# Two attentions beside a stream of expert rows: two query blocks in one turn for tokens 0 to 255

## The chip, the cores and the metric

The kernel runs on one core of one Trainium2 chip. The metric is device microseconds of a whole execution. One execution is also taken with a hardware profiler; its times are measured from the first instruction.

## What is computed

Two blocks on 512 tokens of width 1024, in float32. The first block is a convolution and RWKV mix and then PEER: every token picks 128 of 16384 experts, each with a row of `u` and a row of `v`. The second block is one layer with differential attention (8 heads, two components of 64) and one with latent attention (8 heads), each followed by an MLP with squared ReLU.

```python
def peer_ffn(u, ...):                      # 512 tokens, 8 heads x 16 chosen experts each
    ...
    ue = jnp.take(expert_u, expert, axis=0)
    ve = jnp.take(expert_v, expert, axis=0)
    h = jax.nn.gelu(jnp.einsum('thkd,td->thk', ue, xc).astype(F32), approximate=False)
    return jnp.einsum('thk,thkd->td', (gate * h).astype(xc.dtype), ve)

def diff_attention(hn, ...):
    ...
        s = jnp.einsum('bqhcd,bkhcd->bhcqk', q_blk, k).astype(jnp.float32) * scale
        s = jnp.where(causal_mask(i, S)[None, None, None], s, -jnp.inf)
        p = jax.nn.softmax(s, axis=-1)
        a = p[:, :, 0] - lam * p[:, :, 1]
        return jnp.einsum('bhqk,bkhe->bqhe', a.astype(v.dtype), v)
    ...
def mla_attention(hn, ...):
    ...
        s = (jnp.einsum('bqhd,bkhd->bhqk', qn, k_nope)
             + jnp.einsum('bqhr,bkr->bhqk', qr, k_rope)).astype(jnp.float32) * scale
        s = jnp.where(causal_mask(i, S)[None, None], s, -jnp.inf)
        p = jax.nn.softmax(s, axis=-1)
        return jnp.einsum('bhqk,bkhe->bqhe', p.astype(v.dtype), v)
```

Both attentions are causal in blocks of 128 queries. Query blocks 0 and 1 are tokens 0 to 255, and see 128 and 256 keys.

## The kernel before, in words

Each engine has a program of its own, and engines wait for each other through named semaphores. The part in question begins when the experts of the last 256 tokens are still to be gathered. The second block is run in two halves of 256 tokens. The *first half* (`H.h` = 0) runs beside the expert rows 256 to 511, the *second half* runs alone afterwards.

A *row* is one of the 512 expert slots: GpSimd gathers 128 x 8 KB (line 1748), VectorE forms the dot product with the tokens (L1870), ScalarE applies Gelu, scales, and writes the weights as a diagonal (L1821, L1823, L1828), TensorE adds one half of the product to PSUM (L1767), VectorE the other (L1852). Seven row buffers are in use. Rows are generators, as are the stages of the first half, and `beside` draws from both on each engine:

```python
    def beside(self, stage, rows, rate):
        due = 0.0
        for weight in stage:
            self.turn += 1
            due += rate * (weight or 1)
            while due >= 1:
                next(rows, None)
                due -= 1
```

The rate is 1.1. At one step of the rows' generator ScalarE and VectorE's dot product are at row n+1, VectorE's addition at row n, and TensorE at row n-1. All engines draw the same number of steps after the same piece of a stage, so this is also the order of instructions on each engine. A group of 24 matmuls of an MLP or a projection has weight 1.

An attention stage is `attention`, which every engine runs with its own four functions (line 2126 on). Its blocks are 8 heads x 2 query blocks. In turn n come the scores of block n, the softmax of block n-1, the transposes of block n-2 ("turn") and the product with the values of block n-3 ("meet"); then it yields 1.2. `scores` on TensorE makes one PSUM tile per component in the differential attention (`pe_diff`), one tile in the latent attention (`pe_mla`), each with the causal mask added by a matmul; VectorE takes the maxima (L2428 and L2880) and scales them (L2430, L2882), ScalarE takes the exponentials (L2337, L2766), VectorE normalises (L2437 to L2444, L2887, L2889). `act_turn` copies the transposed block (L2157). At the meet ScalarE copies the output (L2347; L2776, a rounding copy called *put*), squares a finished head (L2350) or VectorE subtracts for the low part (L2895). In the first half only four PSUM banks serve the stages, in rotation (`slot`), and a tile waits until its bank's last reader is done. Exponentials and Gelu need different activation tables, so a load stands in front of each change. The blocks' exponentials have four buffers (`H.E`, `H.mE`), as have the transposed ones (`H.aT`, `H.maT`).

Behind the differential attention come the norm of its heads (matmuls L2280), the projection `w_o_a`, the MLP; then latent attention with `w_o_b` and the second MLP (`pe_mlp`), the final norm (its sums at L1992), and then the second half.

## Time and profile before

| | |
|---|---|
| runs | 3193.8, 3190.64, 3189.07 us, median 3190.64 |
| profiled execution | 3198.6 us, span 3196.8 us |
| TensorE busy | 2730.9 us (85%) |
| VectorE busy | 1994.2 us (62%) |
| GpSimd busy | 1671.4 us (52%) |
| ScalarE busy | 1444.1 us (45%) |
| rows beside the first half | 1350 to 2440 us |
| first half's differential attention | 1533 to 1634 us |
| first half's latent attention | 2049 to 2143 us |

Busy shares over the whole span mix stages with different limits; the sections below read them stage by stage. A mean clock of 1.00 means that TensorE was granted its full 2.4 GHz, 0.50 that it ran at 1.2 GHz. The second half uses the same code, but rows are over by then.

### The profile page before, as it was taken

The numbers are of one execution on the slowest core, as the hardware profiler recorded it, in microseconds if no ns is written. First come the engines' busy times: TensorE is split into PE (matmuls) and PEld (weight loads), VectorE is DVE, ScalarE is ACT, GpSimd is POOL, SyncE is SP. The second block draws the span as 40 slices with busy tenths as digits, with TensorE's granted clock in tenths as the row PEclk, the third lists the DMA queues.
The fourth block names the chain that finished last, engine by engine and source line by source line (L and its number), as shares of the span: only waits on it lengthen the run. The fifth ranks groups of instructions, "written<-read, shape, count | busy, mean of one in ns | idle before, by whom it ended". The sixth has DMA issues, their size and how long they took to land.

```text
span 3196.8 us, 43094 instructions
## 1 busy us (share of the span) xinstructions
PE 2730.9 (85%) x15302; PEld 2099.8 (66%) x15302; DVE 1994.2 (62%) x4229; ACT 1444.1 (45%) x3200; POOL 1671.4 (52%) x1014
## 2 busy tenths in 40 slices
PE   6987997798787778769889998779997999999898
PEld 3856896574333333228557776547876978998898
DVE  5685544477777777667777667767667364255423
ACT  2232222223443343345776555676554355444443
POOL 4822221283344444347447885538884607863675
PEclk8988998899999999989889998889998999999999
DMA  7210001227999999978879998889996505642454
GB/s 287 97 75 1 1 1 53 117 86 300 421 422 421 421 422 420 376 294 346 360 277 370 401 409 331 335 296 379 406 409 273 153 7 165 188 144 78 139 174 124
DMA packets 140517, 797.47 MB, mean 249 GB/s; under 512 B 15504, under 2 KB 18704, under 8 KB 67600
## 3 DMA queue, kind: packets, MB, share of 16 engines
q0 software_dynamic: 73728, 536.90, 41.4%
q1 hardware_dynamic: 65856, 253.36, 22.6%
q10 hardware_dynamic: 720, 4.46, 0.3%
q8 instruction: 123, 2.02, 0.3%
q14 instruction: 90, 0.74, 0.1%
HBM read 788.10 MB, written 6.55 MB: 249 GB/s over the span
## 4 chain that ended last, share of the span: by engine, by line
PE 46%; DMA 15%; DVE 15%; issue 8%; POOL 6%; ACT 5%; DVEq 0%; ACTq 0%; SPq 0%; POOLq 0%
PE ps L2503 8%; PE ps L1767 8%; PE ps L2522 7%; PE ps L876 6%; PE ps L1970 5%; DMA raw<-in_peer_uv,un 4%; POOL wls L299 3%; PE ps L329 3%; DVE scratch L1870 3%; DMA un<-in_peer_uv,un 2%; DMA w<-in_peer_uv,un 2%; DMA w<-in_peer_uv,scratch 2%; DMA un<-in_peer_uv,scratch 2%; POOL wlw L299 1%; POOL raw L1748 1%
## 5 line engine op out<-in xcount | busy, mean ns | idle before, releaser
L299 POOL TENSOR_TENSOR wls<-raws,whs 128x1024 fp32r<-128x1024 f32 (+1 forms) x256 | 613.7, 2407 | 381.4 <-ACT whs L293 376.8
L1767 PE MATMUL ps<-raw,un 128*128 128x512 f32 x730 | 378.7, 637 | 108.1 <-ACT un L1828 107.4
L1821 ACT ACTIVATE un<-un 128x1 f32<-128x1 f32 x512 | 103.5, 202 | 600.7 <-DVE scratch L1870 583.5
L1970 PE MATMUL ps<-ts,whs 128*128 128x256 f32 x1424 | 303.4, 314 | 28.4 <-DVE ts L2060 19.7
L299 POOL TENSOR_TENSOR wlw<-raws,whw 128x1024 fp32r<-128x1024 f32 x112 | 268.0, 2409 | 79.3 <-ACT whw L293 77.9
L1748 POOL DMA_INDIRECT raw<-in_peer_uv,un x205 | 203.3, 992 | 201.7 <-PE ps L1767 128.6
L293 ACT CAST whs<-raws 128x1024 fp32r<-128x1024 f32 (+1 forms) x256 | 263.8, 1036 | 95.8 <-PE ps L2522 34.6
L1767 PEld LDWEIGHTS ps<-raw,un 128*128 128x128 f32 x730 | 132.3, 202 | 251.6 <-ACT un L1828 169.7
L1970 PEld LDWEIGHTS ps<-ts,whs 128*128 128x128 f32 x1424 | 242.1, 205 | 59.8 <-issue 35.5
L2522 PE MATMUL ps<-ts,whs 128*128 128x256 f32 x1216 | 240.7, 299 | 0.0
L1870 DVE SCALAR_TENSOR_TENSOR scratch<-raw,ps 128x1024 f32<-128x1024 f32 x149 | 181.1, 1216 | 94.3 <-DMA raw<-in_peer_uv,un 90.9
L1767 PE MATMUL ps<-un 128*128 128x512 f32 x364 | 197.2, 658 | 45.7 <-ACT un L1828 39.5
L1767 PE MATMUL ps<-w,un 128*128 128x512 f32 x376 | 187.9, 640 | 50.1 <-ACT un L1828 50.1
L1828 ACT ACTIVATE un<-kept,un 128x128 f32<-128x128 f32 x512 | 205.8, 402 | 50.1 <-ACT un L1823 1.9
L2503 PE MATMUL ps<-ts,whw 128*128 128x256 f32 x960 | 192.6, 301 | 20.8 <-DVE ts L2060 20.8
L1970 PE MATMUL ps<-ts,wls 128*128 128x256 f32 x712 | 210.1, 295 | 0.0
L2503 PE MATMUL ps<-ts,whs 128*128 128x256 f32 x1088 | 209.9, 294 | 0.0
L2522 PEld LDWEIGHTS ps<-ts,whs 128*128 128x128 f32 x1216 | 193.4, 192 | 22.2 <-issue 21.5
L299 POOL TENSOR_TENSOR wl<-raw,wh 128x2048 fp32r<-128x2048 f32 x23 | 106.8, 4651 | 171.7 <-ACT wh L293 171.7
L2503 PEld LDWEIGHTS ps<-ts,whs 128*128 128x128 f32 x1088 | 171.4, 191 | 14.9 <-issue 14.2
L2503 PEld LDWEIGHTS ps<-ts,whw 128*128 128x128 f32 x960 | 155.5, 196 | 36.9 <-DVE ts L2060 23.1
L1767 PEld LDWEIGHTS ps<-w,un 128*128 128x128 f32 x376 | 71.7, 202 | 160.8 <-ACT un L1828 92.7
(442 smaller groups left out, 7104.8 us busy)
## 6 DMA issues: line engine op xcount, KB each, us to landing
raws<-in_w_up SPq DMA_DIRECT2D x128, 512.0 KB
raws<-in_w_down SPq DMA_DIRECT2D x128, 512.0 KB
scratch<-in_ada_w SPq DMA_DIRECT2D x17, 1024.0 KB, 13.3
raws<-in_w_qk SPq DMA_DIRECT2D x32, 512.0 KB
raw<-in_w_in SPq DMA_DIRECT2D x11, 1024.0 KB, 6.1
raw<-in_peer_w_q SPq DMA_DIRECT2D x8, 1024.0 KB, 7.9
raws<-in_w_v SPq DMA_DIRECT2D x16, 512.0 KB
raws<-in_w_o_a SPq DMA_DIRECT2D x16, 512.0 KB
```

Of the source, the lines that this page charges most:

```text
L293: e.copy(self.wh[h][:, 0:width], self.raw[slot][:, 0:width]).then_inc(*self.tick("hi", key))
L299: e.tensor_tensor(self.wl[h][:, 0:width], self.raw[slot][:, 0:width], self.wh[h][:, 0:width].bitcast(F32), ALU.subtract).then_inc(*self.ti ...
L329: ins = e.matmul(self.ps[:, b, :], l, r, start=k == 0 and i == 0, stop=k == nk - 1 and i == 2)
L876: ins = e.matmul(self.ps[:, b, 128 * q:128 * q + 128], l, r, start=n == 0, stop=n == len(terms) - 1)
L1748: e.indirect_dma_start(self.rows[r], None, self.d["peer_uv"], index).then_inc(*self.tick(f"row{r}", n, 16))
L1767: ins = e.matmul(self.ps[:, b + half, :], self.diag[n % 4], self.rows[self.row_of(n)][:, 1024 + 512 * half:1536 + 512 * half], start=k == ...
L1821: e.activation(self.gelus[:, c], self.dots[:, c], ACT.Gelu, bias=0.0, scale=1.0).then_inc(*self.tick(S))
L1828: e.activation(self.diag[n % 4], self.C("ident"), ACT.Identity, bias=0.0, scale=self.weight[:, c]).then_inc(*self.tick(S, ("diag", n)))
L1870: e.scalar_tensor_tensor(out=self.junk[n % 2 if n < 256 else 1], in0=self.rows[r][:, 0:1024], scalar=1.0, in1=xn, op0=ALU.mult, op1=ALU.mu ...
L1970: ins = e.matmul(o[:, 0:256], l, r, start=k == 0 and i == 0, stop=k == nk - 1 and i == 2)
L2503: ins = e.matmul(o[:, 0:256], l, r, start=k == 0 and n == 0, stop=k == 7 and n == 2)
L2522: ins = e.matmul(o[:, 0:256], l, r, start=t == 0 and n == 0, stop=t == 3 and n == 2)
```

## The change

For the first half alone, a head's two query blocks go through the attention in one turn. `pairs` has 11 turns of weight 2.4 in place of 19 of weight 1.2. Both blocks' scores of a component lie in one PSUM tile (128 + 256 columns); one wait on either side covers both. The maxima are written side by side and scaled by one instruction; the reciprocals are one instruction. The three transposes of a head go to one PSUM tile and are copied by one instruction of 384 columns; the output of a head is copied (and, in the latent attention, subtracted) in one instruction of 256 columns. Exponentials and normalisations remain one per block and component. The buffers of exponentials serve two heads in place of four blocks. The second half keeps `attention`. Since `beside` draws rows per weight, the rows move as well.

```diff
@@ -2137,8 +2139,48 @@
             yield 1.2
 
     @staticmethod
-    def nothing(n, hh, qb):
+    def nothing(*block):
         return None
+
+    def pairs(self, scores, softmaxed, turn, meet):
+
+        for n in range(11):
+            if n < 8:
+                scores(n)
+            if 1 <= n <= 8:
+                softmaxed(n - 1)
+            if 2 <= n <= 9:
+                turn(n - 2)
+            if n >= 3:
+                meet(n - 3)
+            yield 2.4
+
+    def pe_pair_turn(self, e, S, n, blocks, A_, D_):
+
+        o, before = self.slot((S, "turn", n), (A_, ("turn", n)))
+        for f in before:
+            e.wait_ge(*self.at(*f))
+        e.wait_ge(*self.at(D_, ("soft", n)))
+        for i, a in enumerate((blocks[0][:, 0:128], blocks[1][:, 0:128], blocks[1][:, 128:256])):
+            ins = e.transpose(o[:, 128 * i:128 * i + 128], a, self.C("ident"))
+        ins.then_inc(*self.tick(S, ("turn", n)))
+
+    def act_pair_turn(self, e, S, n, aT, P_):
+        if n >= 2:
+            e.wait_ge(*self.at(P_, ("meet", n - 2)))
+        e.wait_ge(*self.at(P_, ("turn", n)))
+        e.copy(aT, self.bh((P_, "turn", n), 384)).then_inc(*self.tick(S, ("turn", n)))
+
+    def pe_pair_meet(self, e, S, n, v, aT, A_, freed):
+        o, before = self.slot((S, "meet", n), freed)
+        for f in before:
+            e.wait_ge(*self.at(*f))
+        e.wait_ge(*self.at(A_, ("turn", n)))
+        for q, kb in ((0, 0), (1, 0), (1, 1)):
+            c = 128 * (q + kb)
+            ins = e.matmul(o[:, 128 * q:128 * q + 128], v[:, kb, 128 * n:128 * n + 128], aT[:, c:c + 128], start=kb == 0,
+                           stop=kb == q)
+        ins.then_inc(*self.tick(S, ("meet", n)))
...
     def queries(self, H, qb):
...
-        yield from self.attention(H, scores, self.nothing, turn, meet)
+        def pair_scores(n):
+            for c in range(2):
+                p = slice(64 * c, 64 * c + 64)
+                o, freed = self.slot((S, "score", n, c), (A_, ("exp", n, c)))
+                for f in freed:
+                    e.wait_ge(*self.at(*f))
+                if n == 0 and c == 0:
+                    e.wait_ge(*self.at(D_, ("roped", 15)))
+                for qb in range(2):
+                    w, at = 128 * (qb + 1), 128 * qb
+                    e.matmul(o[:, at:at + w], H.q[p, n, 128 * qb:128 * qb + 128], H.k[p, n, 0:w], start=True, stop=False)
+                    ins = e.matmul(o[:, at + 128 * qb:at + w], self.C("ident"), self.C("causal"), start=False, stop=True)
+                ins.then_inc(*self.tick(S, ("score", n, c)))
+
+        def pair_turn(n):
+            self.pe_pair_turn(e, S, n, H.E[2 * (n % 2):2 * (n % 2) + 2], A_, D_)
+
+        def pair_meet(n):
+            if n == 0:
+                e.wait_ge(*self.at(D_, ("w_v", 3, 0)))
+                e.wait_ge(*self.at(A_, ("w_v", 3, 1)))
+            self.pe_pair_meet(e, S, n, H.v, H.aT2[n % 2], A_, (A_, ("o", n)))
+
+        if h:
+            yield from self.attention(H, scores, self.nothing, turn, meet)
+        else:
+            yield from self.pairs(pair_scores, self.nothing, pair_turn, pair_meet)
...
-        yield from self.attention(H, scores, self.nothing, turn, meet)
+        def pair_scores(n):
+            if n == 0:
+                e.wait_ge(*self.at(P_, ("w_v", 3, 1)))
+            if n >= 2:
+                e.wait_ge(*self.at(P_, ("turn", n - 2)))
+            e.wait_ge(*self.at(D_, ("max", n)))
+            st = small[:, 104 + 16 * (n % 2):120 + 16 * (n % 2)]
+            for c in range(2):
+                for qb in range(2):
+                    w, at, i = 128 * (qb + 1), 128 * qb, 8 * c + 4 * qb
+                    e.activation(H.E[2 * (n % 2) + qb][:, 256 * c:256 * c + w],
+                                 self.bh((P_, "score", n, c), at + w)[:, at:at + w], ACT.Exp, bias=st[:, i + 1:i + 2], scale=0.125,
+                                 accum_out=st[:, i + 2:i + 3]).then_inc(*self.tick(S, ("exp", n, c) if qb else None))
+
+        def pair_turn(n):
+            self.act_pair_turn(e, S, n, H.aT2[n % 2], P_)
+
+        def pair_meet(n):
+            e.wait_ge(*self.at(P_, ("meet", n)))
+            e.copy(H.o[:, n, :], self.bh((P_, "meet", n))).then_inc(*self.tick(S, ("o", n)))
+            e.wait_ge(*self.last(S))
+            e.activation(H.q[:, n, :], H.o[:, n, :], ACT.Square, bias=0.0, scale=1.0).then_inc(*self.tick(S, ("sq", n)))
+
+        if h:
+            yield from self.attention(H, scores, self.nothing, turn, meet)
+        else:
...
-        yield from self.attention(H, scores, softmaxed, self.nothing, self.nothing)
+        def pair_scores(n):
+            st = small[:, 104 + 16 * (n % 2):120 + 16 * (n % 2)].rearrange("p (g k) -> p g k", k=4)
+            for c in range(2):
+                e.wait_ge(*self.at(P_, ("score", n, c)))
+                for qb in range(2):
+                    w, at = 128 * (qb + 1), 128 * qb
+                    e.tensor_reduce(st[:, 2 * c + qb, 0:1], self.bh((P_, "score", n, c), at + w)[:, at:at + w], AX,
+                                    ALU.max).then_inc(*self.tick(S))
+            e.wait_ge(*self.last(S))
+            e.tensor_scalar(st[:, :, 1], st[:, :, 0], -0.125, None, ALU.mult).then_inc(*self.tick(S, ("max", n)))
+
+        def pair_softmaxed(n):
+            st = small[:, 104 + 16 * (n % 2):120 + 16 * (n % 2)].rearrange("p (c q k) -> p c q k", q=2, k=4)
+            blocks = [(qb, 128 * (qb + 1), H.E[2 * (n % 2) + qb]) for qb in range(2)]
+            e.wait_ge(*self.at(A_, ("exp", n, 1)))
+            e.reciprocal(st[:, :, :, 3], st[:, :, :, 2]).then_inc(*self.tick(S))
+            e.wait_ge(*self.last(S))
+            e.tensor_scalar(st[:, 1, :, 3], st[:, 1, :, 3], nl, None, ALU.mult).then_inc(*self.tick(S))
+            e.wait_ge(*self.last(S))
+            for qb, w, ee in blocks:
+                e.tensor_scalar(ee[:, 256:256 + w], ee[:, 256:256 + w], st[:, 1, qb, 3:4], None, ALU.mult).then_inc(*self.tick(S))
+            for qb, w, ee in blocks:
+                e.wait_ge(*self.last(S, 1 - qb))
+                e.scalar_tensor_tensor(out=ee[:, 0:w], in0=ee[:, 0:w], scalar=st[:, 0, qb, 3:4], in1=ee[:, 256:256 + w],
+                                       op0=ALU.mult, op1=ALU.add).then_inc(*self.tick(S, ("soft", n) if qb else None))
+
+        if h:
+            yield from self.attention(H, scores, softmaxed, self.nothing, self.nothing)
+        else:
+            yield from self.pairs(pair_scores, pair_softmaxed, self.nothing, self.nothing)
...
-        yield from self.attention(H, scores, self.nothing, turn, meet)
-        yield from self.tail_gemm(e, H, "w_o_b", lambda k: H.A[k], lambda k: (D_, ("put", 2 * k + 1)), S,
...
+            for qb in range(2):
+                w, at, qs = 128 * (qb + 1), 128 * qb, slice(128 * qb, 128 * qb + 128)
+                e.matmul(o[:, at:at + w], H.qn[:, n, qs], H.kn[:, n, 0:w], start=True, stop=False)
+                e.matmul(o[:, at:at + w], H.qr[:, n // 2, qs], H.kr[:, n % 2, 0:w], start=False, stop=False)
+                ins = e.matmul(o[:, at + 128 * qb:at + w], self.C("ident"), self.C("causal"), start=False, stop=True)
+            ins.then_inc(*self.tick(S, ("score", n)))
...
+        if h:
+            yield from self.attention(H, scores, self.nothing, turn, meet)
+        else:
+            yield from self.pairs(pair_scores, self.nothing, pair_turn, pair_meet)
+        yield from self.tail_gemm(e, H, "w_o_b", lambda k: H.A[k], lambda k: (D_, ("put", 2 * k + 1 if h else k)), S,
...
+        def pair_scores(n):
+            st = small[:, 104 + 8 * (n % 2):112 + 8 * (n % 2)]
+            if n >= 2:
+                e.wait_ge(*self.at(P_, ("turn", n - 2)))
+            e.wait_ge(*self.at(D_, ("max", n)))
+            for qb in range(2):
+                w, at = 128 * (qb + 1), 128 * qb
+                e.activation(H.mE[2 * (n % 2) + qb][:, 0:w], self.bh((P_, "score", n), at + w)[:, at:at + w], ACT.Exp,
+                             bias=st[:, 4 * qb + 1:4 * qb + 2], scale=192.0 ** -0.5,
+                             accum_out=st[:, 4 * qb + 2:4 * qb + 3]).then_inc(*self.tick(S, ("exp", n) if qb else None))
...
     def dve_mla(self, e, H):
...
+        def pair_scores(n):
+            st = small[:, 104 + 8 * (n % 2):112 + 8 * (n % 2)].rearrange("p (q k) -> p q k", k=4)
+            e.wait_ge(*self.at(P_, ("score", n)))
+            for qb in range(2):
+                w, at = 128 * (qb + 1), 128 * qb
+                e.tensor_reduce(st[:, qb, 0:1], self.bh((P_, "score", n), at + w)[:, at:at + w], AX,
+                                ALU.max).then_inc(*self.tick(S))
+            e.wait_ge(*self.last(S))
+            e.tensor_scalar(st[:, :, 1], st[:, :, 0], -(192.0 ** -0.5), None, ALU.mult).then_inc(*self.tick(S, ("max", n)))
...
+        def pair_softmaxed(n):
+            st = small[:, 104 + 8 * (n % 2):112 + 8 * (n % 2)].rearrange("p (q k) -> p q k", k=4)
+            e.wait_ge(*self.at(A_, ("exp", n)))
+            e.reciprocal(st[:, :, 3], st[:, :, 2]).then_inc(*self.tick(S))
+            e.wait_ge(*self.last(S))
+            for qb in range(2):
+                w, ee = 128 * (qb + 1), H.mE[2 * (n % 2) + qb]
+                e.tensor_scalar(ee[:, 0:w], ee[:, 0:w], st[:, qb, 3:4], None,
+                                ALU.mult).then_inc(*self.tick(S, ("soft", n) if qb else None))
+
+        def pair_meet(n):
+            e.wait_ge(*self.at(A_, ("put", n)))
+            e.tensor_tensor(H.A[n][1], self.bh((P_, "meet", n)), H.A[n][0].bitcast(F32),
+                            ALU.subtract).then_inc(*self.tick(S, ("put", n)))
+
+        if h:
+            yield from self.attention(H, scores, softmaxed, self.nothing, meet)
+        else:
+            yield from self.pairs(pair_scores, pair_softmaxed, self.nothing, pair_meet)
```

ScalarE's instructions in the middle of the first half's differential attention. `e` are exponentials, `at` and `ap` the transposed blocks, `o` and `q` the output and its squares; L1821, L1823 and L1828 together are a row. Before, a turn of a 128-key block:

```order
L2337 ACT_TABLE_LOAD
L2337 ACTIVATE e_111,kept<-ps,kept 128x128 x2
L2157 COPY at_113<-ps 128x128
L2347 COPY o_100<-ps 128x128
L2350 ACTIVATE q_97<-o_100 128x256
L1821 ACT_TABLE_LOAD
L1821 ACTIVATE un<-un 128x1
L1823 ACTIVATE un<-un 128x1
L1828 ACTIVATE un<-kept,un 128x128
```

After the change, from the load to the second row of the same turn:

```order
L2430 ACT_TABLE_LOAD
L2430 ACTIVATE e_109,kept<-ps,kept 128x128
L2430 ACTIVATE e_110,kept<-ps,kept 128x256
L2430 ACTIVATE e_109,kept<-ps,kept 128x128
L2430 ACTIVATE e_110,kept<-ps,kept 128x256
L2172 COPY ap_117<-ps 128x384
L2439 COPY o_100<-ps 128x256
L2441 ACTIVATE q_97<-o_100 128x256
L1821 ACT_TABLE_LOAD
L1821 ACTIVATE un<-un 128x1
L1823 ACTIVATE un<-un 128x1
L1828 ACTIVATE un<-kept,un 128x128
```

Four exponentials now stand behind one load, and two or three rows behind the other. The whole program has 74 table loads where it had 106.

TensorE in the same place (L1767 is a row, L2258 and L2259 or L2325 and L2326 scores and mask, L2152 or L2165 transposes, L2166 or L2181 the product with the values). Before:

```order
L2258 MATMUL ps<-k_98,q_97 128x256
L2259 MATMUL ps<-kept 128x128
L2258 MATMUL ps<-k_98,q_97 128x256
L2259 MATMUL ps<-kept 128x128
L2152 MATMUL ps<-kept,e_112 128x128 x2
L2166 MATMUL ps<-at_115,v_99 128x128
L1767 MATMUL ps<-scratch,un 128x512
L2258 MATMUL ps<-k_98,q_97 128x128
```

After:

```order
L2326 MATMUL ps<-kept 128x128
L2165 MATMUL ps<-kept,e_111 128x128
L2165 MATMUL ps<-kept,e_112 128x128 x2
L2181 MATMUL ps<-ap_117,v_99 128x128 x3
L1767 MATMUL ps<-un 128x512 x2
L1767 MATMUL ps<-raw_64,un 128x512
L2325 MATMUL ps<-k_98,q_97 128x128
L2326 MATMUL ps<-kept 128x128
```

Where one row stood between two turns' scores, three stand here.

TensorE at the last row. Before, in `mlp1` (L2522, its last value matmuls) and the final norm:

```order
L2522 MATMUL ps<-ts_90,whw_83 128x256 x2
L2522 MATMUL ps<-ts_90,wlw_84 128x256
L1767 MATMUL ps<-raw_64,un 128x512
L1992 MATMUL ps<-gel_91,kept 128x256
L1787 MATMUL ps<-kept,un 128x128 x8
```

After:

```order
L2645 MATMUL ps<-ts_90,whw_83 128x256 x2
L2645 MATMUL ps<-ts_90,wlw_84 128x256
L1767 MATMUL ps<-raw_64,un 128x512
L2645 MATMUL ps<-ts_90,whw_83 128x256 x2
L2645 MATMUL ps<-ts_90,wlw_84 128x256
```

The last row has moved ahead of the MLP's last 180 matmuls.

## Rows read from the trace of the kernel before

**Rows 1.** The page's first line.

```profile
span 3196.8 us, 43094 instructions
```

**Rows 2.** Stretches: from:to, length, busy us and instructions per engine, clock, DMA share, GB/s.

```profile
1541.70:1624.00 82.30, 65.83 (x208) 36.24 (x209) 63.93 (x190) 73.48 (x173) 17.85 (x19) 0.77 0.83 321
2054.00:2134.00 80.00, 51.98 (x183) 31.20 (x181) 50.67 (x130) 69.68 (x149) 20.39 (x22) 0.84 0.85 321
2200.00:2400.00 200.00, 191.70 (x1300) 163.05 (x1299) 134.81 (x261) 111.77 (x261) 167.13 (x103) 1.00 1.01 406
2680.00:2840.00 160.00, 160.00 (x1335) 160.00 (x1334) 44.70 (x113) 73.74 (x110) 128.69 (x55) 1.00 0.60 183
```

**Rows 3.** Line L2337, 1534 to 1636 us: ns min/median/max, first and last start.

```profile
L2337 ACT ACT_TABLE_LOAD  x16: 1283/1283/1283, 1537.2 to 1623.1; - x16
```

**Rows 4.** Line L2766, 2049 to 2146 us.

```profile
L2766 ACT ACT_TABLE_LOAD  x16: 1283/1283/1283, 2053.1 to 2132.2; - x16
```

**Rows 5.** ScalarE in order of time, first stage: start, us taken, instruction.

```profile
1580.23 0.47 ACT L2337 ACTIVATE e<-ps,kept 128x256 f32<-128x256 f32 x1
...
1581.14 0.37 ACT L2157 COPY at<-ps 128x256 f32<-128x256 f32 x1
1581.39 0.28 ACT L2347 COPY o<-ps 128x128 f32<-128x128 f32 x1
1581.69 1.28 ACT L1821 ACT_TABLE_LOAD   x1
1582.99 0.20 ACT L1821 ACTIVATE un<-un 128x1 f32<-128x1 f32 x1
...
1584.04 0.20 ACT L1821 ACTIVATE un<-un 128x1 f32<-128x1 f32 x1
...
1586.43 0.37 ACT L2337 ACTIVATE e<-ps,kept 128x128 f32<-128x128 f32 x1
...
1587.13 0.26 ACT L2157 COPY at<-ps 128x128 f32<-128x128 f32 x1
```

**Rows 6.** VectorE in order of time, first stage; in brackets the idle time before.

```profile
1600.20 0.75 DVE L1852 SCALAR_TENSOR_TENSOR ps<-un,ps 128x512 f32<-128x512 f32 x1 [0.66 <-ACT un L1823]
1600.86 0.42 DVE L2428 TENSOR_REDUCE kept<-ps 128x1 f32<-128x256 f32 x1
1601.31 0.15 DVE L2430 TENSOR_SCALAR kept<-kept 128x1 f32<-128x1 f32 x1
...
1602.40 0.29 DVE L2442 TENSOR_SCALAR e<-e,kept 128x128 f32<-128x128 f32 x1
...
1602.99 1.21 DVE L1870 SCALAR_TENSOR_TENSOR scratch<-raw,ps 128x1024 f32<-128x1024 f32 x1
...
1604.13 0.75 DVE L1852 SCALAR_TENSOR_TENSOR ps<-un,ps 128x512 f32<-128x512 f32 x1
```

**Rows 7.** TensorE in order of time, first stage, at the lower and the upper clock.

```profile
1543.67 0.79 PE L2258 MATMUL ps<-k,q 64*128 64x128 f32 x2
1544.39 0.79 PE L2259 MATMUL ps<-kept 128*128 128x128 f32 x2
...
1596.82 1.02 PE L1767 MATMUL ps<-scratch,un 128*128 128x512 f32 x2
1597.78 0.70 PE L2258 MATMUL ps<-k,q 64*128 64x256 f32 x2
1598.40 0.49 PE L2259 MATMUL ps<-kept 128*128 128x128 f32 x2
1598.82 0.70 PE L2258 MATMUL ps<-k,q 64*128 64x256 f32 x2
```

**Rows 8.** VectorE in order of time, second stage: the subtraction behind the put.

```profile
2095.07 0.29 DVE L2895 TENSOR_TENSOR ts<-ps,ts 128x128 fp32r<-128x128 f32 x1 [1.73 <-ACT ts L2776]
```

**Rows 9.** TensorE in order of time: the first matmuls behind the two stages.

```profile
1636.68 0.60 PE L2280 MATMUL ps<-q,kept 128*8 128x256 f32 x2
...
2143.36 0.80 PE L1970 MATMUL ps<-ts,whs 128*128 128x256 f32 x2
```

**Rows 10.** TensorE in order of time, where the rows end.

```profile
2437.88 1.02 PE L1767 MATMUL ps<-raw,un 128*128 128x512 f32 x2
2444.02 1.22 PE L1992 MATMUL ps<-gel,kept 128*128 128x256 f32 x2 [5.12 <-DVE gel L2051]
```

26 lines of the change are left out of this document (24 added, 2 removed).

## The prediction

> **What bounds the kernel now.** I read first the table of stretches: the two attention stages of the first half of the tokens (1533 to 1634 us and 2049 to 2143 us), the expert rows beside the MLP (2200 to 2400) and the same MLP code in the second half, without rows (2680 to 2840). Beside the MLP the DMA engines are full (share 1.01, 406 GB/s) and TensorE is busy 191.7 of 200 us; in the two attention stages ScalarE is the fullest engine (73.48 of 82.3 us and 69.68 of 80 us), the DMA share is 0.83 and 0.85, and the mean TensorE clock is 0.77 and 0.84 [rows 2]. Then I read the pace of the attention turns: sixteen Exp table loads from 1537.2 to 1623.1 us are 15 gaps of 5.73 us; in the second stage 2053.1 to 2132.2 gives 5.27 us [rows 3, 4]. Then one turn of ScalarE: two exponentials of 256 columns 0.91 us (1580.23 to 1581.14), two copies 0.55 (to 1581.69), a table load 1.30 to the next start (to 1582.99), a row's three activations 1.05 (to 1584.04), and at 128 columns the exponentials take 0.70 (1586.43 to 1587.13) [rows 5]. With the Exp load of 1.30 that is 5.1 us for a turn with one row and 6.2 with two, which is the measured pace: the first stage runs at ScalarE's sum, half of it table loads. The second adds a loop through VectorE, which waits 1.73 us in a turn for ScalarE's cast [rows 8].
>
> The program's time is 3198.6 us for a span of 3196.8 [rows 1]; sums are made against 3198.6, and their result is taken off the median of the runs, 3190.6, which lies 8 us lower.
>
> **The change, part by part.** Per attention stage, 19 turns of weight 1.2 become 11 of weight 2.4. At 1.1 rows per weight the stage carries 29 rows instead of 25. The rows are drawn after a turn's work, so they now stand in bunches of 3 or 2 where there were 1 or 2. Between the eight Exp loads of the first stage they are 3, 2, 3, 3, 2, 3, 3, and in the second 2, 3, 3, 2, 3, 3, 2.
>
> *ScalarE's own sum.* A pair of turns costs 2 x 5.73 = 11.5 us. A joint turn keeps all exponentials (0.91 + 0.70), has one load of each table (2.6), one copy of 384 and one of 256 columns (an estimate of 0.66 from 0.28 to 0.37 us for 128 and 256 columns [rows 5]), the square (0.43) and 2.64 rows at 1.05 (2.8): 8.1 us. All in all 32 table loads go. What a load costs is the 1.30 us from its start to the next activation's [rows 5]. The Trainium skill, page "ScalarE: Activation LUTs", section "What ACT_TABLE_LOAD costs", adds about 1.38 us of drain to each 1.28 us load. By that 32 loads would give back some 44 us more, as an estimate from the page; the trace does not agree, since the activation behind the load starts 1.30 us after it and the copy before it ends as it starts, so nothing is counted for it.
>
> *What is late next: the first stage.* TensorE works two rows behind ScalarE. In a bunch of two both its rows were made ready in the turn before, but the third of a bunch needs the diagonal that ScalarE makes first in this same bunch, behind load, exponentials, copies and the Gelu load. On TensorE the next turn's scores are queued behind it. From the moment the maxima are ready: 1.3 + 1.6 + 1.1 + 1.3 + 1.0 = 6.3 us to that diagonal; its matmul 0.96 (1596.82 to 1597.78); the scores, per component 0.42 and 0.62 us for 128 and 256 columns and 0.42 twice for the mask, 1.87, twice 3.74 [rows 7]; the last maximum and its scaling, with handovers, 1.0 (0.42 and 0.15 are the ops [rows 6]). That is 12.0 us at the upper clock level. While it waits TensorE stands still for 4 us in a row, and at the lower level a step of 0.42 takes 0.72 (1543.67 to 1544.39) [rows 7]. I add 1.0 for part of the scores at that level: 13.0. A bunch of two is bound by VectorE, which waits for the weight of the bunch's first row, as it does today for 0.66 us behind a table load [rows 6]: 5.8 + 0.66 + 1.4 for maxima = 7.9, taken 8.2. Seven gaps: 5 x 13.0 + 2 x 8.2 = 81.4 against 85.9 [rows 3]: -4.5. Bounds: VectorE's path alone (9.7 and 7.9) gives 64.3, -21.6; the lower clock throughout (15.6 and 10.3) gives 98.6, +12.7.
>
> *The first stage's end.* From the last maxima to the matmuls of the sub-norm (1636.68 [rows 9]) stand four turns' rows and those of the weight 2 behind: 7.5 rows now, 12.8 then. Now it is 13.0 us, and VectorE does a row in 1.80 us (1.14 from 1602.99 to 1604.13 and 0.66 behind it [rows 6]). 5.3 more rows are 9.5 us; waiting once for ScalarE and the wider last softmax, with its 128-column part at 0.59 us (1602.40 to 1602.99 [rows 6]), 2.9 more. A row is 128 x 8 KB, 2.6 us at 406 GB/s [rows 2], and twelve in a line outrun it: +2 (0 to 8). The first maxima come 2 us later, since a component now has both blocks' scores ahead of them. Stage: -4.5 + 12.4 + 2 + 2 = +11.9.
>
> *The second stage.* No scores wait for an exponential's bank here, and they are 1.8 us a pair. The loop is ScalarE to the put (1.3 + 0.8 + 0.65 = 2.75), the joint subtraction 0.35, rows at 1.80, maxima and scaling 0.85: 9.4 for three rows, 7.5 for two; by TensorE's third row 5.0 + 0.96 + 1.8 + 0.9 = 8.7 and up to 10.7 at the lower clock. I take 9.9 and 7.5: 4 x 9.9 + 3 x 7.5 = 62.1 against 79.1 [rows 4]: -17.0 (-20 to -12). Its end, from the last maxima at 2132 to the first matmul of w_o_b at 2143.36 [rows 9], is 11.3 us now with 5.3 rows and 22.8 with 10.6, two of them hidden behind the put: +11.4; +1.3 for start and supply. Stage: -4.3.
>
> *The second MLP's end.* Both stages take 8 rows off it: behind the last row TensorE has 180 weight matmuls where it had none, 7.5 groups of 24. With rows a group takes 4.03 us (1300 records in 200 us, 108 of them rows'), without 2.88 (1335 in 160) [rows 2]: 7.5 x 1.15 = -8.6. At the seam the norm's sums start 6.0 us after the last value matmul (2437.9 to 2444.02 [rows 10]); the last row's VectorE work (1.8) and its sums' copy on ScalarE leave that wait, the slow adds beside GpSimd stay: -3.4 (0 to -4.5). Together -12.0.
>
> *Nothing* is counted for the second half, whose attention is untouched, for the stores of keys and values (same place), and for GpSimd's splits, which follow the same spots. If more rows per turn made GpSimd issue late, the DMA's free share in the stages (0.83, 0.85) covers some 15% and no more.
>
> Sum: +11.9 - 4.3 - 12.0 = **-4.4 us**, 3194.2 on the profiled execution's scale and 3186 on the runs'.
>
> **Rivals.** *A, the third row holds nobody.* If TensorE's last row of a bunch finds its diagonal ready, or its delay is hidden by VectorE, the first stage runs on VectorE's path, 17 us less: 3169. For it: VectorE's sum is itself 8 to 9.7, and ScalarE's 8.1. Against: ScalarE can't reach the row before two loads. *B, TensorE's clock makes it slower.* The still stretches of 4 us in five of seven turns keep the clock at its lower level while the scores, now on the path, run: +17 in the first stage and +4 in the second, 3207. For it: the level is lower already for almost half of the first stage (0.77) [rows 2]. It is slower than before from 13.9 us per three-row turn on. Against: TensorE is busy for 8 us behind each wait. *C, the merged work does not matter,* because rows keep the pace by DMA: at 2.6 us a row the stage's 29 rows need 75 us, less than the 100 it takes, so only ends and starts are touched; 3194. That the change doesn't do what it says is ruled out by the order of instructions: 74 table loads stand where 106 stood.
>
> **How the numbers follow.** My forecast 0.50, A 0.24, B 0.18, C 0.08. A measurement tells about 0.2%, 6.4 us, from no change. The forecast's own spread (3179 to 3195) lies one third beyond -6.4. So faster 0.24 + 0.17 = 0.41; slower 0.18 + 0.02 = 0.20; the same 0.39. The range, 3168 to 3204, leaves out 0.2 at its ends.
>
> **What would show it.** In the changed kernel's first stage: Exp loads 12 to 13.5 us apart where three rows lie between, 8 where two do; TensorE idle for 3 to 4 us before the third row of a bunch, with ScalarE's diagonal as the releaser; ScalarE no longer over 90% busy; VectorE working rows back to back for over 20 us behind the last exponential; in the second stage 9.9 and 7.5. The last row about 20 us before the second MLP's end. If the three-row gaps are under 11 us the third row is not the bound and A holds; if over 14, B. It is wrong as a whole if the MLP's matmuls after the last row don't run at 2.9 us per 24.

## The result: slower, because the next scores queue behind a late row and then run at the lower clock

The changed kernel takes 3209.3 us (median of 13 runs, 3198.7 to 3214.2) where the kernel before takes 3198.3 (13 runs, 3189.1 to 3205.2): 1.0028 times as long, 95% interval 1.0018 to 1.0039. I had forecast a gain of 4.4 us, to 3186 us, starting from the 3190.6 us that the first three runs of the kernel before gave; its thirteen runs give 3198.3, so 7.7 of the 23 us between 3186 and 3209.3 are not of the change, and the changes themselves, -4.4 and +9 us, are compared below. The profiled execution took 3211.3 us against 3198.6. Of all runs behind this document one is set aside, 5262.8 us for e12, whose other five lie between 3159.7 and 3169.3 with a median of 3166.3.

Page of the changed kernel, its first lines; the busy times beside those of the table before the change:

```profile
span 3209.5 us, 42886 instructions
...
PE 2739.1 (85%) x15302; PEld 2111.0 (66%) x15302; DVE 1984.3 (62%) x4149; ACT 1398.6 (44%) x3136; POOL 1676.0 (52%) x1014
```

ScalarE is indeed 45 us less busy (1444.1 before), 41 of them its 32 table loads of 1.28 us, and the kernel is slower all the same. To see where, I followed instructions that both kernels have and noted how much later each starts:

| instruction | before | after | later by | in this piece | forecast |
|---|---|---|---|---|---|
| projections ahead of the first stage | 1435.8 | 1440.9 | 5.1 | | |
| first matmul of the sub-norm | 1636.7 | 1660.6 | 24.0 | +18.9 | +11.9 |
| first MLP's start (L2503) | 1684.2 | 1711.0 | 26.8 | +2.8 | 0 |
| ahead of the second stage | 2048.2 | 2068.0 | 19.8 | -7.0 | 0 |
| first matmul of `w_o_b` | 2143.4 | 2165.6 | 22.2 | +2.4 | -4.3 |
| last value matmul of the second MLP | 2438.0 | 2451.8 | 13.8 | -8.4 | -8.6 |
| behind the seam | 2501.6 | 2514.0 | 12.4 | -1.4 | -3.4 |

The 5.1 us ahead of the stage is in code that the change doesn't touch, and is scatter of executions: in ten of the twelve kernels below the same place is 2.4 to 6.6 us later than in this execution of before, in two 0.8 and 1.2. What is left is +7.3 us, which agrees with the ratio's 9 within the interval's 3. Forecast were -4.4. Both attention stages are worse than forecast by 7 us each, and the MLP's end is right.

The loads of the Exp table in the changed kernel, first and second stage (number of loads, first and last start; before: [rows 3, 4]):

```profile
L2430 ACT ACT_TABLE_LOAD  x8: 1283/1283/1283, 1543.7 to 1635.7; - x8
...
its engine sat idle before it (us, times) until:
  DVE kept L2556: 28.7, 6
```

```profile
L2933 ACT ACT_TABLE_LOAD  x8: 1283/1283/1283, 2073.4 to 2140.8; - x8
```

Seven gaps take 92.0 us in the first stage (14.3, 7.9, 15.4, 15.5, 8.1, 16.1, 14.6) and 67.4 in the second (5.5, 12.8, 10.7, 7.7, 12.0, 11.0, 7.7). The short ones are those with two rows (and the first of the second stage, 5.5). ScalarE, 89% busy in the stage before (73.48 of 82.30 us [rows 2]), now sits idle for 28.7 us ahead of its loads until VectorE has the scaled maxima (the profile names L2556, the instruction next to the scaling L2550). Who is it that makes them late? One turn of three rows, first ScalarE:

```profile
1581.36 1.28 ACT L2430 ACT_TABLE_LOAD   x1 [7.22 <-DVE kept L2556]
...
1585.48 1.28 ACT L1821 ACT_TABLE_LOAD   x1
...
1587.39 0.40 ACT L1828 ACTIVATE un<-kept,un 128x128 f32<-128x128 f32 x1
...
1596.87 1.28 ACT L2430 ACT_TABLE_LOAD   x1 [6.59 <-DVE kept L2556]
```

TensorE in the same turn (start, us taken, in brackets the idle time ahead of the instruction and what ended it):

```profile
1582.12 3.37 PE L1767 MATMUL ps<-un 128*128 128x512 f32 x4
1587.85 1.44 PE L1767 MATMUL ps<-raw,un 128*128 128x512 f32 x2 [2.35 <-ACT un L1828]
1589.22 0.79 PE L2325 MATMUL ps<-k,q 64*128 64x128 f32 x2
1589.94 0.79 PE L2326 MATMUL ps<-kept 128*128 128x128 f32 x2
...
1595.13 0.79 PE L2326 MATMUL ps<-kept 128*128 128x128 f32 x2
1595.72 0.85 PE L2165 MATMUL ps<-kept,e 128*128 128x128 f32 x3
```

Two rows run at 1582.12, the third only at 1587.85, when ScalarE has made its diagonal (L1828, 1587.39), and the next scores behind it from 1589.22 to 1595.72. A step of 128 columns takes 0.72 us (1589.22 to 1589.94), what it took at the lower clock level before [rows 7]. The stretches of these scores in the first and in the second stage (columns as in [rows 2]; the granted clock is the third number from the end):

```profile
1589.20:1595.70 6.50, 6.50 (x17) 4.06 (x17) 1.31 (x5) 0.90 (x3) 0.94 (x1) 0.50 0.81 308
2117.50:2120.80 3.30, 3.30 (x13) 2.94 (x12) 1.24 (x3) 0.90 (x3) 0.94 (x1) 0.50 0.97 340
```

Both ran at 0.50, 1.2 GHz, behind a row for which TensorE had stood idle. So did the scores of the other three-row turns of the first stage: 0.50 over three of them, 0.57 over the last (1628.6 to 1634.5), behind waits of 3.4 to 4.9 us. In the second stage the other three read 0.65 to 0.71. Behind the two rows of a short turn the scores ran at 1.00 and 0.98 (1600.0 to 1603.7, 1561.1 to 1564.7).

### The profile page after: what moved, and what is told of

It is laid out like the page before. It is cut to its first block, busy times and chain, and to the rows that moved or that the text cites. A ratio compares the mean times of both kernels' runs of the same rounds, so it can differ in the third digit from the quotient of the medians.

```text
span 3209.5 us, 42886 instructions
## 1 busy us (share of the span) xinstructions
PE 2739.1 (85%) x15302; PEld 2111.0 (66%) x15302; DVE 1984.3 (62%) x4149; ACT 1398.6 (44%) x3136; POOL 1676.0 (52%) x1014
## 4 chain that ended last, share of the span: by engine, by line
PE 48%; DMA 14%; DVE 14%; POOL 7%; issue 6%; ACT 5%; DVEq 0%; ACTq 0%; SPq 0%; POOLq 0%
PE ps L1767 8%; PE ps L2645 7%; PE ps L2626 7%; PE ps L876 6%; PE ps L1972 6%; DMA raw<-in_peer_uv,un 4%; POOL wls L299 3%; PE ps L329 3%; DMA un<-in_peer_uv,un 3%; DVE scratch L1870 2%; DMA raw<-in_peer_uv,scratch 2%; DMA w<-in_peer_uv,un 2%; POOL wlw L299 1%; DMA w<-in_peer_uv,scratch 1%; DMA un<-in_peer_uv,scratch 1%
## 5 line engine op out<-in xcount | busy, mean ns | idle before, releaser
L1767 PE MATMUL ps<-raw,un 128*128 128x512 f32 x730 | 381.7, 643 | 114.5 <-ACT un L1828 113.4
L1821 ACT ACTIVATE un<-un 128x1 f32<-128x1 f32 x512 | 103.4, 202 | 597.7 <-DVE scratch L1870 586.1
L1972 PE MATMUL ps<-ts,whs 128*128 128x256 f32 x1424 | 304.9, 315 | 27.5 <-DVE ts L2062 18.9
L1767 PEld LDWEIGHTS ps<-raw,un 128*128 128x128 f32 x730 | 133.9, 203 | 263.8 <-ACT un L1828 174.4
L1767 PE MATMUL ps<-un 128*128 128x512 f32 x364 | 194.4, 652 | 64.7 <-ACT un L1828 61.2
L1767 PE MATMUL ps<-w,un 128*128 128x512 f32 x376 | 188.6, 642 | 51.2 <-ACT un L1828 51.1
L1828 ACT ACTIVATE un<-kept,un 128x128 f32<-128x128 f32 x512 | 205.8, 402 | 48.6 <-ACT un L1823 1.5
L2626 PEld LDWEIGHTS ps<-ts,whs 128*128 128x128 f32 x1088 | 172.4, 192 | 15.3 <-issue 14.1
L2725 DVE TENSOR_TENSOR kept<-kept,ps 128x256 f32<-128x256 f32 x256 | 104.0, 417 | 123.4 <-PE ps L2645 123.1
```

The lines of the kernel that those rows point to most:

```text
L1767: ins = e.matmul(self.ps[:, b + half, :], self.diag[n % 4], self.rows[self.row_of(n)][:, 1024 + 512 * half:1536 + 512 * half], start=k == ...
L1821: e.activation(self.gelus[:, c], self.dots[:, c], ACT.Gelu, bias=0.0, scale=1.0).then_inc(*self.tick(S))
L1828: e.activation(self.diag[n % 4], self.C("ident"), ACT.Identity, bias=0.0, scale=self.weight[:, c]).then_inc(*self.tick(S, ("diag", n)))
L1972: ins = e.matmul(o[:, 0:256], l, r, start=k == 0 and i == 0, stop=k == nk - 1 and i == 2)
L2626: ins = e.matmul(o[:, 0:256], l, r, start=k == 0 and n == 0, stop=k == 7 and n == 2)
L2725: e.tensor_tensor(x, x, self.bh((P_, "v", g, j)), ALU.add).then_inc(*self.tick(S, ("x", g, j)))
```

## Experiments

Each is stated against the kernel before, which ran beside it on the same chip (4 to 12 runs each); medians of before lay between 3199.0 and 3200.8 us. Where the text compares two of these kernels, or one of them with the changed kernel, it takes their medians; by the ratios such a difference can come out about 2 us smaller.

| kernel | median us | ratio, 95% |
|---|---|---|
| e1: joint turns in the first stage alone | 3216.8 | 1.0056 (1.0041 to 1.0071) |
| e2: joint turns in the second stage alone | 3198.8 | 0.9995 (0.9981 to 1.0008) |
| e3: scores ahead of the rows on TensorE | 3179.8 | 0.9942 (0.9927 to 0.9957) |
| e4: TensorE kept busy while it waits | 3198.2 | 1.0000 (0.9989 to 1.0012) |
| e5: the kernel before, with the moved rows | 3201.6 | 1.0003 (0.9994 to 1.0013) |
| e6: two rows a turn | 3180.6 | 0.9945 (0.9929 to 0.9962) |
| e7: e3 with transposes earlier too | 3176.8 | 0.9931 (0.9914 to 0.9949) |
| e8: rows drawn at two places of a turn | 3201.6 | 1.0005 (0.9996 to 1.0014) |
| e9: e7 and two rows a turn | 3182.8 | 0.9950 (0.9935 to 0.9965) |
| e10: e7 with few rows in the last turns | 3180.6 | 0.9937 (0.9920 to 0.9955) |
| e11: e9 with rate 1.13 | 3171.8 | 0.9918 (0.9901 to 0.9936) |
| e12: two rows a turn, rate 1.13, order as changed | 3166.6 | 0.9903 (0.9884 to 0.9922) |

### Which stage: e1 and e2

For one of the attentions the branch of the second half is taken in both halves:

```diff
-        if h:
+        if True:
             yield from self.attention(H, scores, self.nothing, turn, meet)
```

> The joint turns in the differential attention alone; the latent attention has its 19 single turns as before. The profiled changed kernel lost 18.9 us up to the end of the first stage, gave 6.7 back in the MLP behind it, and lost 2.4 net in the second stage. If the losses add up stage by stage, this kernel ends 8 to 12 us behind the kernel before (the MLP's end gives back half of what it gave, since only 4 rows are moved ahead). If the give-back in the first MLP is DMA work caught up, it is seen here too, 5 to 8 us. If the 4 rows moved are what counts, this kernel and the one with the second stage alone come out alike.

> The joint turns in the latent attention alone. If the stages add up: second stage +2, the end of the second MLP -5 (4 rows instead of 8 moved ahead of it), so 1 to 5 us ahead of the kernel before. If bunching itself costs something outside its stage (late gathers), it is no better than the kernel before.

e2 can't be told from the kernel before, and so does not choose between its two expectations. e1 is much worse than expected: 18 us behind the kernel before where 8 to 12 were. The stage itself repeats (+20.4 us in e1, +18.9 in the changed kernel), so the loss is the first stage's. The surprise is the second MLP: with 8 rows moved ahead of its end the changed kernel gained 8.4 us there, with 4 rows e1 gained 0.9 and e2 1.8, not half. So the two parts don't add up (+0.56% and -0.05% against +0.28% for both). Why four rows bring so little I didn't find out.

### What the third row's place costs: e3

TensorE alone puts the next head's scores ahead of the rows; the order of its other instructions, and the rotation of PSUM banks, stay.

```diff
+            if n < 8 and not (ahead and n):
                 scores(n)
...
                 meet(n - 3)
+            if ahead and n < 7:
+                scores(n + 1)
             yield 2.4
```

> The changed kernel, with TensorE's order alone altered: the scores of the next head stand ahead of a turn's rows, not behind them. ScalarE and VectorE keep their order. Theory (TensorE's third row waits for ScalarE's diagonal, the next scores are queued behind it and then run at the lower clock): the three-row gaps between Exp loads fall from 15.3 to about 10 us in the first stage and from 11.7 to about 9.5 in the second, the wait before the third row goes, the clock of the first stage rises from 0.71 to over 0.85, and the kernel is 30 us faster than the changed one, some 20 us faster than before. Rival (rows come late from the gathers, or VectorE's order is the bound): the gaps fall by under 2 us each and the kernel stays at or behind the kernel before.

It is 0.58% faster than before (18.6 us), 29.5 us faster than the changed kernel (medians), as the theory said. The loads of its first stage and TensorE in one turn:

```profile
L2432 ACT ACT_TABLE_LOAD  x8: 1283/1283/1283, 1543.1 to 1613.9; - x8
```

```profile
1596.42 0.49 PE L2327 MATMUL ps<-k,q 64*128 64x128 f32 x2 [0.33 <-ACT e L2432]
...
1599.76 0.49 PE L2328 MATMUL ps<-kept 128*128 128x128 f32 x2
1600.08 1.02 PE L1767 MATMUL ps<-raw,un 128*128 128x512 f32 x2
1600.94 1.02 PE L1767 MATMUL ps<-scratch,un 128*128 128x512 f32 x2
1601.80 1.02 PE L1767 MATMUL ps<-un 128*128 128x512 f32 x2
```

```profile
1596.40:1600.00 3.60, 3.58 (x16) 2.32 (x17) 0.86 (x2) 3.51 (x10) 0.00 (x0) 1.00 0.99 357
```

The gaps sum to 70.8 us instead of 92.0 (59.8 instead of 67.4 in the second stage). The scores take 3.7 us at the full clock, three rows follow without a wait. One part of what I expected failed: the stage's mean clock rose from 0.72 to 0.81 only; it still reads 0.50 from 1559 to 1574 and for about 5 us each from 1589, 1609 and 1624.

And two gaps did not move, the first with three rows in each stage: 14.3 us, as in the changed kernel, and 12.1 (12.8 there). VectorE waits there for the gathers of its rows, 3.43 and 4.27 us in the first stage, 3.08 and 1.86 in the second, and its maxima stand behind these rows:

```profile
1555.11 1.22 DVE L1870 SCALAR_TENSOR_TENSOR scratch<-raw,ps 128x1024 f32<-128x1024 f32 x1 [4.27 <-DMA raw<-in_peer_uv,un]
...
1556.91 1.14 DVE L2549 TENSOR_REDUCE kept<-ps 128x1 f32<-128x128 f32 x4
```

The changed kernel has the same waits (4.26 us at 1555.7, 3.96 at 2085.4), so in these two turns late gathers alone would have held the turn nearly as long.

### What of it is the clock: e4

Ahead of a bunch's third row TensorE runs five matmuls of 256 columns into the tile that the next scores overwrite.

```diff
             while due >= 1:
+                if drawn == 2 and self.fill:
+                    self.fill()
                 next(rows, None)
...
+                for _ in range(5):
+                    e.matmul(o[:, 128:384], H.q[0:64, n - 1, 128:256], H.k[0:64, n - 1, 0:256], start=True, stop=True)
```

> The changed kernel, with five matmuls of 256 columns added on TensorE ahead of the third row of a bunch, while it waits (they write the tile that the next scores overwrite, so they change nothing else). If the lower clock is what stretches the scores from 3.74 to 6.5 us, TensorE now keeps the upper level, the three-row gaps of the first stage fall from 15.3 to 12.5 to 13.5 us, and the whole falls by 8 to 15 us though work was added. If the clock is not the cause, the gaps stay at 15.3 or grow by up to 1 us.

With work added the kernel fell by 11 us (9 by the ratios), to the time of the kernel before. TensorE in one such turn; L1773 is the row, L2345 the added work:

```profile
1604.19 2.42 PE L2345 MATMUL ps<-k,q 64*128 64x256 f32 x10
1606.78 1.12 PE L1773 MATMUL ps<-un 128*128 128x512 f32 x2 [0.17 <-ACT un L1834]
1607.84 0.48 PE L2333 MATMUL ps<-k,q 64*128 64x128 f32 x2
...
1611.17 0.49 PE L2334 MATMUL ps<-kept 128*128 128x128 f32 x2
1611.50 0.49 PE L2173 MATMUL ps<-kept,e 128*128 128x128 f32 x3
```

The scores take 3.7 us (1607.84 to 1611.50) instead of 6.5. Its gaps are 13.8, 8.1, 15.4, 12.3, 8.1, 12.3, 14.7 in the first stage: in two of the five three-row turns the scores ran at 1.00, and these take 12.3; in the other three they ran at 0.50 to 0.55 all the same. In the second stage the seven gaps take 60.7 us instead of 67.4. So the same order costs 12.3 us a turn at the upper level and 15.4 at the lower; e3, with the order mended, 9.1 to 11.3 behind its first turn. That splits the excess of a three-row turn: about 3 us are the clock, 1 to 3 the order.

### The moved rows by themselves: e5

```diff
-            yield 1.2
+            yield 1.2 if H.h else 1.39
```

> The kernel before with its single turns, their weight 1.39 in place of 1.2 in the first half: 29 rows instead of 25 in each stage, singly and in twos, and the last row ahead of the second MLP's last 180 matmuls, as in the changed kernel. By the terms of my sum: a row more costs a stage ScalarE's 1.05 us, so +4 to +5 in each stage, about +3 at each stage's end (VectorE's 1.8 us a row), and the second MLP's end gives 8.6 back: 3 to 8 us slower than before. If moving rows forward is worth more than it costs, it is faster by 2 to 5 us.

No difference (+0.03%, interval -0.06 to +0.13), which is neither of the two expectations. In the profile the gaps of the stages grow by 2.4 and 6.3 us and their ends by 1.9 each, 12.5 in all, and the second MLP is 7.5 us shorter, the first 5 (of which, as shown further below, 3 may be scatter). So the rows that a stage takes on are paid back behind it. The loss isn't the four rows; it is how they stand.

### No third row: e6 and e8

```diff
-            yield 2.4
+            yield 1.82
```

> The changed kernel with the joint turn's weight 1.82 in place of 2.4: exactly two rows behind each turn, 22 rows a stage, none that is a third of its bunch; six rows fewer than before stand in the stages, and they stand behind the second MLP. If the third row is what makes a turn long, all gaps between Exp loads are near 8.0 us, the first stage is 35 to 45 us shorter than in the changed kernel (its end 4 to 5 of that), the second 15 to 20, the rows left behind the MLP cost 11 to 16 us and the MLP's row-free tail of 8.6 is lost: 20 to 35 us faster than the changed kernel. If joint turns are long for another reason (clock, supply, VectorE), the gaps are 10 us and more and it is slower than the changed kernel.

```diff
                 softmaxed(n - 1)
+            yield 1.2
             if 2 <= n <= 9:
...
                 meet(n - 3)
-            yield 2.4
+            yield 1.2
```

> The changed kernel with the turn's weight given in two parts of 1.2, one ahead of the transposes and products and one behind them: the same 29 rows, but in ones and twos, never three in a row. If the bunch as such is what costs, the gaps fall to 9 or 10 us and the whole by 20 us or more. If it is the wait of TensorE's third row of a turn for the diagonal that ScalarE makes first in the same turn, wherever it stands, only the copies (1.3 us) leave that wait: the three-row gaps fall from 15.3 to 14 us, the whole by 3 to 10 us against the changed kernel.

e6 has no third row in a turn, and is 28.7 us faster than the changed kernel. Its loads:

```profile
L2430 ACT ACT_TABLE_LOAD  x8: 1283/1283/1283, 1543.3 to 1603.6; - x8
```

The gaps are 7.3, 11.8, 7.3, 8.1, 9.0, 8.1, 8.7, together 60.3. The scores of the long one did run at the lower level, but they were done at 1559.4, and what VectorE's maxima (1561.06) wait for is a gather that comes 2.85 us late:

```profile
1559.25 1.22 DVE L1870 SCALAR_TENSOR_TENSOR scratch<-raw,ps 128x1024 f32<-128x1024 f32 x1 [2.85 <-DMA raw<-in_peer_uv,un]
```

In the second stage five of seven are 9.3 or 7.7. A third row in a turn had thus made it 7 us longer in the first stage, 4 in the second. The first stage is 36 us shorter than in the changed kernel, as expected, the second 22, somewhat more. (The profiled execution, 3167.3 us, is the fastest of e6's six; their median is 3180.6.)

e8 keeps all 29 rows but never three in a row. It gained 8 us on the changed kernel. Its gaps in the first stage are 13.9, 8.2, 15.1, 11.4, 7.4, 15.3, 11.4: in the turns of 15.1 and 15.3 TensorE still waits 4.3 and 3.5 us for ScalarE's diagonal and runs the scores at the lower level; in the two of 11.4 it keeps the upper one, which I had not expected (14 us for all of them). The wait of the first:

```profile
1566.74 2.08 PE L1767 MATMUL ps<-scratch,un 128*128 128x512 f32 x2 [4.30 <-ACT un L1823]
1568.75 0.79 PE L2326 MATMUL ps<-k,q 64*128 64x128 f32 x2
```

So it is the dependence within a turn, not the bunch.

### What bounds the mended turn: e7, e9 and e10

e7 also puts a head's transposes one turn earlier on TensorE, behind the scores:

```diff
+            if ahead and 1 <= n <= 8:
+                turn(n - 1)
             yield 2.4
```

> The kernel with the scores ahead of the rows (3179.8 us), and on TensorE the transposes of a head one turn earlier, behind the next head's scores and ahead of the rows. There ScalarE waited 1.48 us in a turn with its Exp table loaded, until TensorE had done the transposes behind the last rows, and VectorE 2.88 us for ScalarE. If that wait is on the path, the three-row gaps fall from 9.1 to 11.3 to about 9.7 and less, 1 to 1.5 us a turn in both stages together 8 to 12 us. If VectorE's own sum (9.4 to 9.7 us) is the bound already, under 3 us.

> Both remedies at once: scores and transposes ahead of the rows on TensorE, and two rows behind each joint turn (22 a stage). If two-row turns of 8 us are ScalarE's sum (two loads, exponentials, copies, two rows: 7.6 us), only the turns of 9.0 and 11.8 us in the first stage of the two-row kernel, where TensorE ran at its lower level, get shorter: 2 to 8 us faster than 3180.6. If VectorE's wait for the transposes and weights counts too, 10 us and more. If the rows left to the MLPs are paced by the DMA engines, nothing.

e10 is e7 with

```diff
-            yield 2.4
+            yield 2.73 if n < 8 else 0.91
```

> The kernel with scores and transposes ahead of the rows (3176.8 us), its first eight turns with weight 2.73 (three rows each) and the last three, which have no new scores, with 0.91 (one row each): 27 rows a stage, 8 instead of 12 to 13 behind the last maxima. By VectorE's 1.8 us a row the stages' ends fall from 28.3 and 24.6 to about 20 and 17 us, the two gaps of 7.7 grow to 9.7, and four rows more beside the second MLP cost 4.3: 2 to 8 us faster. If the ends are not VectorE's rows, no change.

e7 can't be told from e3 (the intervals overlap). Its three-row gaps behind the first turn are 9.1 to 10.0: VectorE's sum of three rows, softmax and maxima, the second of the two expectations. e9 gained nothing on e6: its first-stage gaps (7.9, 11.7, 7.4, 8.1, 8.7, 8.2, 8.2) are the same, the long second one too, where VectorE waits 2.68 us for a gather. With two rows a turn the order no longer matters.

e10 missed. The ends did fall, from 28.3 and 24.6 us to 17.2 and 14.1, but the kernel didn't get faster than e7 (3180.6 and 3176.8 us). The gaps grew by 2.5 and 6.7, the second MLP by 6.4 us. Rows taken out of the uncovered end are paid for where they go.

### A better version: e11 and e12

```diff
-RATE = 1.1
+RATE = 1.13
...
-            yield 2.4
+            yield 1.775
```

This is e12 against the changed kernel; e11 is e9 with the same two numbers.

> The same with the general rate 1.13 instead of 1.1 and the joint turn's weight 1.775 (still two rows a turn): the six rows that stood behind the second MLP are spread over projections and MLPs, and the last row stands at the MLP's end, as before the change. If the MLPs' pace is that of the DMA engines, which carry every row somewhere, only the bare rows behind the MLP go: 3 to 8 us faster than the same kernel with rate 1.1. If a row more costs an MLP the 2.6 us that it takes at 406 GB/s, the gain is nothing or a loss of up to 6 us.

> The changed kernel with two numbers altered and its order kept: the joint turn's weight 1.775 (two rows a turn) and the general rate 1.13. Two-row turns have no third row, and the orders with and without the early scores came out alike at two rows (3182.8 and 3180.6 us), so this should equal the kernel with both (3171.8 us) within 0.2%. If the early scores still shorten turns once the rows are spread anew, it is 6 us or more behind that kernel.

e6 and e9 leave six rows behind the second MLP, where nothing covers them. With the rate at 1.13 they stand beside projections and MLPs. e11 gained 11 us on e9, more than the 3 to 8 expected, and e12, the changed kernel with only these two numbers altered, is at 3166.6 us the fastest: 0.97% faster than before (interval 0.78 to 1.16), and not told apart from e11 (their intervals overlap). Its loads in both stages:

```profile
L2430 ACT ACT_TABLE_LOAD  x8: 1283/1283/1283, 1543.6 to 1602.3; - x8
```

```profile
L2933 ACT ACT_TABLE_LOAD  x8: 1283/1283/1283, 2037.6 to 2087.6; - x8
```

Gaps of 58.7 and 50.0 us in sum, against 86.0 and 79.0 before, with 22 rows in each stage where before had 25. So the joint turn with two rows and the rate 1.13 is a good change; with the weight that came with it, it was not. How much of the 0.97% is the joint turn's is not shown: the single turns with rate 1.13 and fewer rows in the stages were not run. e5 shows only that more rows in the stages gain them nothing.

## Right and wrong, step by step

**ScalarE's sum: right.** The exponentials, copies and loads up to the second table load took 4.1 us (1581.36 to 1585.48; forecast 1.3 + 1.6 + 1.1). In a turn with two rows ScalarE is busy for 7.1 of 8.1 us (1596.87 to 1604.97); my terms, 8.1 us for 2.64 rows, give 7.4 for two. So its sum is right, and it is nearly the bound of a two-row turn, as VectorE's path is.

**The third row waits: right, in place and size.** From the load to the row's start 6.5 us (forecast 6.3 to the diagonal), the scores queued behind. TensorE is idle ahead of the third row for 4.8, 4.7, 2.35, 4.9 and 3.4 us in the five turns of the first stage, 4.0 on average (forecast 3 to 4); the turn shown above has the shortest, since its first two rows took 3.37 us at the lower clock.

**Two-row gaps: right.** 7.9 and 8.1 us in the first stage (8.2), 5.5, 7.7, 7.7 in the second (7.5).

**Three-row gaps: the step that failed.** I wrote the path at the upper clock level, 12.0, and added "1.0 for part of the scores at that level". The scores ran at the lower one, in four of the five turns from first to last and in the fifth but for their first microsecond. The terms as measured in the turn shown: 6.5 to the diagonal, 1.4 the row's matmul (0.96), 6.5 the scores (3.74 + 1.0), 1.15 maxima and scaling (1.0), in sum 15.5. The five gaps average 15.2, so the stage's gaps are 92.0, not 81.4: 10.6 us of the whole distance of 11.7 between forecast and result. The second stage's gaps add 5.3 (67.4 against 62.1), and the other misses take 4.2 off. The order of the step was right and its size was not: the term of the scores, 4.7 us forecast, measured 6.5. This is rival B, for whose gaps I had 15.6; its two-row gaps of 10.3 didn't come. It gave 3207, as change +16, where +9 was measured. I gave it 0.18, and argued that TensorE is busy for 8 us behind each wait. It was busy, but at the lower level: the clock came back only when the scores were over (it reads 0.50 up to 1598 and 1.00 from 1599 on). In the second stage the turn with the slowest scores has 5.6 to the diagonal's use, 1.9 the row (0.96), 3.4 the scores (1.8), 1.15, in sum 12.0, where I took 9.9. The four three-row gaps average 11.6; one of them, 12.8, is one of the two with late gathers, where VectorE waits 3.96 and 1.65 us for its rows. I had counted nothing for gathers between the loads of a stage; the other such turn is the first of the first stage, 14.3.

**The stages' ends: right in the first, short by 2 in the second.** 25.0 us now and 13.5 before, +11.5 where I had 12.4 and 2 for the gathers; 24.8 and 11.2, +13.6, in the second, where I had 11.4. VectorE works its rows back to back, 1.80 us apart:

```profile
1645.82 1.21 DVE L1870 SCALAR_TENSOR_TENSOR scratch<-raw,ps 128x1024 f32<-128x1024 f32 x1
...
1647.62 1.21 DVE L1870 SCALAR_TENSOR_TENSOR scratch<-raw,ps 128x1024 f32<-128x1024 f32 x1
...
1657.24 1.22 DVE L1870 SCALAR_TENSOR_TENSOR scratch<-un,ps 128x1024 f32<-128x1024 f32 x1 [0.53 <-DMA un<-in_peer_uv,un]
```

At the stage's end the gathers are late for the last three rows only, by half a microsecond each: the 2 us for them was not needed there.

**The second MLP's end: right.** 180 weight matmuls without rows in 21.60 us, 2.88 for 24, as forecast:

```profile
2430.20:2451.80 21.60, 21.55 (x180) 21.35 (x179) 9.32 (x21) 8.11 (x13) 8.88 (x5) 1.00 0.25 74
```

**The seam: wrong.** The whole seam gave 1.4 us where I had 3.4. From the last value matmul to the norm's sums it is 6.5 us now and 6.0 before. What is there are not the row's operations but VectorE's additions while GpSimd works through four splits in a row:

```profile
2451.04 2.25 DVE L2053 TENSOR_TENSOR gel<-gel,gel 128x256 f32<-128x256 f32 x1
2453.22 0.41 DVE L2725 TENSOR_TENSOR kept<-kept,ps 128x256 f32<-128x256 f32 x1
2453.55 4.71 DVE L2053 TENSOR_TENSOR gel<-gel,gel 128x256 f32<-128x256 f32 x2
```

```profile
2447.92 10.05 POOL L299 TENSOR_TENSOR wls<-raws,whs 128x1024 fp32r<-128x1024 f32 x4 [12.39 <-ACT whs L293]
```

Such an addition takes 0.42 us a little earlier (2446.37), 2.25 and more during the splits. Before, three splits stood there. That GpSimd's work slows them is read from their coincidence and wasn't tried. The Trainium skill ("GPSIMD Engine Reference", "Specifications") says that GpSimd contends with VectorE's instructions that have two SBUF inputs; the rows agree, since the addition from PSUM between them keeps its 0.41 us. The gain is behind the sums, on ScalarE, as forecast: VectorE's next step starts 1.7 us after them (2458.31 to 2460.05) and 3.1 before the change (2444.02 to 2447.15), where the last row's copy and a table load stood in between.

**Not in the forecast:** the first MLP and the projections behind it, 7.0 us shorter than in the execution of before. From the first MLP's start to the second stage's first load it is 368.9 us before and 362.4 after; e2, which has before's code up to there, took 365.7, and e6, e7, e9 and e10, with the changed kernel's code and rate there, 359.2 to 365.4. The scatter is as large as the effect, and I claim no cause.

**Rival A** (the third row holds nobody, 3169) fell as a description of the changed kernel, but it describes e3, where the order frees the row: three of the four later three-row gaps are 9.1 to 9.9 us, the path of VectorE that I had put at 9.7. **Rival C** (rows keep the DMA's pace) fell for the stages as wholes with e3, which ran through the two in 26 us less with the same 58 rows; it holds for the first three-row turn of each stage, whose gap e3 left at 14.3 and 12.1 us.

**The drain of a table load:** of the Trainium skill's 1.38 us beside each load ("ScalarE: Activation LUTs", "What ACT_TABLE_LOAD costs") the changed kernel shows nothing either: in the rows above, the second load starts at 1585.48, right behind the square, and three activations later the diagonal starts 1.91 us after it.

## What to carry to other kernels

Work that is drawn by weight moves when weights are merged: before merging turns, write down for each engine which item of the bunch depends on something that another engine makes in the same turn, and what is queued behind it; either order the queue so that the critical work stands ahead, or keep the bunch as short as the lag between the engines. When a path goes through TensorE behind waits like these (2.35 to 4.9 us), try the sum with its work at the lower clock, whole: that would have given 15.6 here, and 15.2 was measured. And an edit that saves an engine's time can be right while the constants that came with it are wrong: here two numbers turned +0.28% into -0.97%. Which turns a remedy leaves as they were is worth a look too: here they showed the late gathers.
